# Third LayerNorm and pre-norm in one pass over the un-normed sum, with four projections multiplied before the norm and corrected when they are copied out

## The chip, the cores and the metric

The kernel runs on one core of a Trainium2 chip. The metric is the device time of one launch in microseconds (us); the time of a version is the median of its runs. Five engines work from queues of their own, each in program order: TensorE (PE, with its weight loads listed as PEld), VectorE (DVE), ScalarE (ACT), GpSimd (POOL) and SyncE (SP, which here only issues loads). They wait for each other by semaphores.

## The reference, cut to what matters

Two transformer blocks follow each other on 256 tokens of 1024 channels. The change lies at the seam.

```python
def layer_norm(x, g, b):
    xf = x.astype(f32)
    mu = xf.mean(-1, keepdims=True)
    var = jnp.square(xf - mu).mean(-1, keepdims=True)
    return ((xf - mu) * lax.rsqrt(var + EPS) * g.astype(f32) + b.astype(f32)).astype(x.dtype)
...
def rms_norm(x, g):
    x32 = x.astype(jnp.float32)
    y = x32 * lax.rsqrt(jnp.mean(x32 * x32, axis=-1, keepdims=True) + NORM_EPS)
    return (y * g.astype(jnp.float32)).astype(x.dtype)
...
        h = conv_ffn(x, ffn_w_up[l], ffn_conv_w[l], ffn_conv_b[l], ffn_w_down[l])
        x = layer_norm(ALPHA * x + h, ln3_g[l], ln3_b[l])
...
    h = rms_norm(x, g_pre_mix) * (1 + scale1) + shift1
    (sc_b, sc_c, sc_x, q, k, v, z, xbc, dt_raw,
     gl_a, gl_b, gl_c) = split_columns(h @ w_in)
```

`shift1` and `scale1` are columns of a modulation `silu(c) @ mod_w + mod_b`.

## The kernel before, in words

Activations lie with channels on the partitions and the 256 tokens along the columns: `X` is eight k-tiles of 128 x 256. Every large product is made from float32r halves: an operand is split into a rounded high half and the low rest, and `three` (L415) issues three matmuls, high by high, low by high, high by low. One unit of a linear (`linears_g`, L435) makes 256 output channels: 8 k-tiles x 2 column halves x 3 matmuls of 256 columns, 48 in all, into one of three PSUM banks (`lin`); five other banks (`att`) rotate for everything else.

Weights come through a plan (L187 to L291), a list of 512 KB pieces in the order of their use. `load` (L309) puts a piece into one of six raw buffers by SP. `stage` (L337) makes its halves: the high one on ScalarE (`hir`), the low one on VectorE (`lor`), in four buffers of each. `take` (L381) stages up to three pieces ahead of the one that PE is about to use, as far as buffers are free. Between weight pieces the plan carries 48 modulation pieces (`add_mod`); each is one multiply with a sum over 1024 columns on VectorE (`mod_step`, L331). All helpers append to the queue of an engine at once (`Queue.do`, L64), so the order of the Python code is the order of each engine's work, and a wait blocks what stands behind it on that engine alone.

The first block ends with eleven gated units "up" (convolution, gelu, product, split by `hid_put`) and four units "down" of 22 k-tiles (L1137 to L1140). After each "down" unit `resid` adds the result to `X`, and `stats` collects sums and squares. Then `layer_norm` (L1166) runs: `finish` (L932) turns the sums into mean and 1/deviation on small tiles and spreads them over the partitions with a diagonal and a matmul by ones; `apply` (L963) subtracts, scales, squares for the next norm and writes `X`. `pre_norm` (L1180) does the same for the RMS norm and splits the result h1 into high and low halves in `INH` and `INL`. Only then can PE start the units of the second block: q and k together (L1212), the small dt product (L1217), v, xs0, xs1, bc with a convolution of 2.4 us on VectorE behind each of the last three, scc, scx (L1276 to L1282), scb, z0, z1, and then the attention and scan stage with the gate units as filler.

Of the kernel before, what the change touches and what calls it, by code (L numbers as in the profile page):

```python
# [93 lines left out]
def build(nc, A, out):  # L94
    with ExitStack() as ctx:
# [14 lines left out]
        INH = sb("INH", 2048, F32R)[:, :].rearrange("p (k t) -> p k t", t=T)  # L110
        INL = sb("INL", 2048, F32R)[:, :].rearrange("p (k t) -> p k t", t=T)
# [149 lines left out]
        for c in range(4):  # L261
            add(("down", c), A["ffn_w_down"], 256 * c, 22, mod=3, spread=True)
# [4 lines left out]
        for n in ("v", "xs0", "xs1", "bc", "scc", "scx", "scb", "z0", "z1"):  # L267
            add((n, 2), w2, P2[n], 8, mod=int(n[0] in "sz"))
# [886 lines left out]
        def square3(k, n, d, t):  # L1155

            b = k // 2 % 2
            s_ = SQ[:, b, (k % 2) * T:(k % 2 + n) * T].rearrange("p (b t) -> p b t", t=T)
            for i in range(n):
                h = act(s_[:, i, :], d[:, i, :], ACT.Square, t, *sqf[b], scale=V("ln3_g", k + i), bias=V("ln3_b", k + i))  # L1160
            if k % 2 or n == 2:
                fold()
                sqp["fold"] = k // 2, h
            return h
# [498 lines left out]
```

How the kernel before makes its waits and increments, by code:

```python
    def wait(self, *tokens):  # L53
        need = {}
        for t in tokens:
            if t is not None:
                k = id(t[0])
                if t[1] > self.seen.get(k, 0) and t[1] > need.get(k, (None, 0))[1]:
                    need[k] = t
        for k, (sem, v) in need.items():
            self.seen[k] = v
            self.todo.append(lambda e, s=sem, v=v: e.wait_ge(s, v))
# [1 line left out]
    def do(self, fn, *tokens, inc=True):  # L64
        self.wait(*tokens)
        if not inc:
            self.todo.append(fn)
            return None
        self.n += 1
        self.todo.append(lambda e: fn(e).then_inc(self.sem, 1))
        return (self.sem, self.n)
# [101 lines left out]
        def dma(o, i, *w, s=None, q=None):  # L173
            if s is None:
                nsem[0] += 1
                s = sem(f"s_d{nsem[0]}")
            q = q or SP
            q.wait(*w)
            q.todo.append(lambda e: e.dma_start(o, i).then_inc(s, 16))
            return (s, 16)
```

## Time and profile before

| what | value |
|---|---|
| median of 3 runs | 922.96 us (922.44 to 923.41) |
| the profiled execution's own time | 921.22 us |
| its span, first to last instruction | 919.4 us |
| mean granted TensorE clock | 0.960 of full |
| busy: PE, DVE, ACT | 859.9, 647.6, 486.9 us |
| moved by DMA | 166.40 MB, 181 GB/s on average |

The rows further down are read so: in a timeline the first number is the start in us from the beginning of the span, the second the time to the end of the last instruction of a merged group, `out<-in` are the tiles, `xN` the number of instructions, and the bracket tells how long the engine was idle before and what ended that. Durations of neighbours overlap a little, so the distance of two starts is the better measure of what one costs.

### The profile page before, as it was taken

How to read it: one execution, taken by the hardware profiler on the slowest of the kernel's cores; microseconds unless marked ns; L12 is line 12 of the kernel's file. 1: busy time of each engine (PE TensorE's matmuls, PEld its weight loads, DVE VectorE, ACT ScalarE, POOL GpSimd, SP SyncE). 2: the span in 40 equal slices, each digit the busy share in tenths (PEclk: the TensorE clock that was granted, in tenths of full speed). 3: DMA queues.
4: the chain of work that ended last, by engine and by line, in shares of the span. 5: the costliest groups of instructions: out<-in, count | busy, mean ns of one | idle time of the engine just before them, and what ended most of it. 6: DMA issues, size and time to landing. Idle time of an engine off the chain costs nothing.

```text
span 919.4 us, 16216 instructions
## 1 busy us (share of the span) xinstructions
PE 859.9 (94%) x6578; PEld 821.4 (89%) x6578; DVE 647.6 (70%) x986; ACT 486.9 (53%) x680; POOL 6.2 (1%) x15
## 2 busy tenths in 40 slices
PE   5999998989889999999968999999996999999995
PEld 5889986879779999999967999898995999999995
DVE  4775777688678877787766696677877766655443
ACT  5644447444445666654435646788654544444450
POOL 0200000000000000000000000000000000000000
PEclk9999999989999999999977999999997899999998
DMA  9774556846052766569851485564664377765531
GB/s 332 219 234 124 180 180 190 250 155 229 25 161 91 218 185 180 182 189 318 267 182 46 134 264 167 143 187 142 219 192 138 104 240 230 228 208 170 178 111 47
DMA packets 145578, 166.40 MB, mean 181 GB/s; under 512 B 5488, under 2 KB 135536, under 8 KB 145504
## 3 DMA queue, kind: packets, MB, share of 16 engines
q1 hardware_dynamic: 143888, 162.82, 57.0%
q0 software_dynamic: 544, 1.49, 0.7%
q8 instruction: 52, 0.85, 0.4%
q10 hardware_dynamic: 1072, 1.05, 0.3%
q14 instruction: 22, 0.18, 0.1%
HBM read 164.10 MB, written 1.25 MB: 180 GB/s over the span
## 4 chain that ended last, share of the span: by engine, by line
PE 71%; DVE 8%; ACT 4%; issue 1%; DVEq 0%; ACTq 0%
PE ps L166 48%; PE ps L421 22%; DVE X L145 2%; ACT FA L142 2%; DVE lor L145 1%; DVE FA L145 1%; ACT hir L142 1%; ACT L142 1%; DVE FA L149 1%; DVE INL L145 1%; DVE st L145 0%; PE ps L169 0%; ACT SQ L142 0%; DVE X L153 0%; DVE SQ L145 0%
## 5 line engine op out<-in xcount | busy, mean ns | idle before, releaser
L166 PE MATMUL ps<-INH,hir 128*128 128x256 f32 x1320 | 384.4, 291 | 15.9 <-DVE lor L145 10.8
L145 DVE TENSOR_TENSOR lor<-raw,hir 128x1024 fp32r<-128x1024 f32 (+1 forms) x268 | 310.3, 1174 | 123.7 <-ACT hir L142 109.1
L421 PE MATMUL ps<-INL,hir 128*128 128x256 f32 x1320 | 379.4, 287 | 1.2 <-DVE INL L145 0.8
L166 PE MATMUL ps<-INH,lor 128*128 128x256 f32 x1320 | 378.7, 287 | 0.0
L142 ACT ACTIVATE hir<-raw 128x1024 fp32r<-128x1024 f32 (+1 forms) x268 | 266.9, 1015 | 143.4 <-PE ps L421 134.9
L166 PEld LDWEIGHTS ps<-INH,hir 128*128 128x128 f32 x1320 | 258.7, 196 | 23.8 <-issue 11.8
L421 PEld LDWEIGHTS ps<-INL,hir 128*128 128x128 f32 x1320 | 258.4, 196 | 2.8 <-DVE INL L145 2.8
L166 PEld LDWEIGHTS ps<-INH,lor 128*128 128x128 f32 x1320 | 258.8, 196 | 1.1 <-issue 1.0
L166 PE MATMUL ps<-HIH,hir 128*128 128x256 f32 x608 | 173.7, 286 | 0.2 <-DVE lor L145 0.2
L166 PE MATMUL ps<-HIH,lor 128*128 128x256 f32 x608 | 172.0, 283 | 0.0
L421 PE MATMUL ps<-HIL,hir 128*128 128x256 f32 x608 | 172.0, 283 | 0.0
L166 PEld LDWEIGHTS ps<-HIH,hir 128*128 128x128 f32 x608 | 116.6, 192 | 2.1 <-issue 1.2
L166 PEld LDWEIGHTS ps<-HIH,lor 128*128 128x128 f32 x608 | 116.7, 192 | 0.5 <-issue 0.5
L421 PEld LDWEIGHTS ps<-HIL,hir 128*128 128x128 f32 x608 | 116.7, 192 | 0.0
L153 DVE SCALAR_TENSOR_TENSOR FA<-ps,vec,FA 128x254 f32<-128x254 f32 (+2 forms) x130 | 53.2, 473 | 20.9 <-ACT FA L142 20.7
L142 ACT ACT_TABLE_LOAD x43 | 55.2, 1283 | 8.6 <-DVE small L156 5.5
L334 DVE SCALAR_TENSOR_TENSOR raw<-raw,cb 128x1024 f32<-128x1024 f32 x48 | 58.2, 1218 | 0.0
L142 ACT ACTIVATE FA<-ps,vec 128x256 f32<-128x256 f32 x58 | 29.4, 558 | 40.4 <-PE ps L421 40.4
L142 ACT ACTIVATE FA<-ps 128x512 f32<-128x512 f32 x47 | 27.4, 594 | 36.9 <-PE ps L421 30.7
L166 PE MATMUL ps<-FA 128*128 128x256 f32 (+6 forms) x212 | 39.2, 365 | 3.5 <-DVE FA L145 2.7
L142 ACT ACTIVATE HIH<-FA 128x512 fp32r<-128x512 f32 (+2 forms) x34 | 21.3, 628 | 39.3 <-DVE FA L145 17.4
L145 DVE TENSOR_TENSOR HIL<-FA,HIH 128x512 fp32r<-128x512 f32 (+2 forms) x34 | 23.4, 689 | 23.0 <-ACT HIH L142 22.9
(128 smaller groups left out, 634.6 us busy)
## 6 DMA issues: line engine op xcount, KB each, us to landing
raw<-in_w_in SPq DMA_DIRECT2D x64, 512.0 KB, 4.6
raw<-in_mod_wT SPq DMA_DIRECT2D x48, 512.0 KB, 4.5
raw<-in_ffn_w_up SPq DMA_DIRECT2D x44, 512.0 KB, 4.5
raw<-in_w_ffn_in SPq DMA_DIRECT2D x44, 512.0 KB, 4.7
raw<-in_ffn_w_down SPq DMA_DIRECT2D x20, 512.0 KB, 4.8
raw<-in_w_ffn_out SPq DMA_DIRECT2D x20, 512.0 KB, 3.4
raw<-in_xa_wkv SPq DMA_DIRECT2D x16, 512.0 KB, 4.0
raw<-in_xa_wq SPq DMA_DIRECT2D x8, 512.0 KB, 5.3
```

Of the source, the lines that this page charges most:

```text
L142: return AC.do(lambda e: e.activation(o, i, f, **kw), *w)
L145: return DV.do(lambda e: e.tensor_tensor(o, a, b, op), *w)
L149: return DV.do(lambda e: e.tensor_scalar(o, a, s1, None, op0), *w)
L153: return DV.do(lambda e: e.scalar_tensor_tensor(out=o, in0=a, scalar=s, in1=b, op0=op0, op1=op1), *w)
L166: return PE.do(lambda e: e.matmul(o, l, r, start=start, stop=stop, skip_group_check=True), *w, inc=inc)
L334: return DV.do(lambda e: e.scalar_tensor_tensor(out=w, in0=w, scalar=1.0, in1=CB[:, :], op0=ALU.mult, op1=ALU.mult, accum_out=col), t, t_sc)
L421: return PE.do(lambda e: e.matmul(o, *b, start=False, stop=stop, skip_group_check=True), inc=stop)
```

## The change

The statistics of the sum `ALPHA*x + h` now serve both norms: besides sum and square sum, products with the LayerNorm's gain and bias give the RMS of the normed result by algebra (`sums`, `rows3`). While the "down" units run, each tile of `X` is scaled by the combined gain (`GG`) and split into `INH` and `INL` un-normed, with four extra columns (gain, bias, shift) behind the 256 (`put_scaled`, `vector`). The units q, k, scc and scx multiply that (`late_g`; each holds two banks), and are corrected when they are copied out: `centre` subtracts the mean's share and scales by 1/deviation, `settle` applies the RMS factor and the shift. The true h1 is still made for dt, v and all later units (`h1_put`, `h1_low`), now in `HIH` and `HIL`. The units scc and scx move ahead of dt and v; six modulation pieces move from the "down" units to the kv units, and two from scc and scx to xs0 and xs1. The small constants and one matmul that sums three of them over the partitions come ahead of the "down" units.

The diff, cut to its core (`diag` is the first half of `spread`, and `steps_of` runs a number of a generator's steps):

```diff
+        INHX = sb("INH", 8 * TE, F32R)[:, :].rearrange("p (k t) -> p k t", t=TE)
+        INLX = sb("INL", 8 * TE, F32R)[:, :].rearrange("p (k t) -> p k t", t=TE)
+        INH, INL = INHX[:, :, 0:T], INLX[:, :, 0:T]
         HIH = sb("HIH", 22 * T, F32R)[:, :].rearrange("p (k t) -> p k t", t=T)
         HIL = sb("HIL", 22 * T, F32R)[:, :].rearrange("p (k t) -> p k t", t=T)
         SQ = sb("SQ", 1024)[:, :].rearrange("p (a n) -> p a n", a=2)
-            add(("kv", c), A["xa_wkv"], 256 * c, 8, mod=1)
+            add(("kv", c), A["xa_wkv"], 256 * c, 8, mod=2)
-            add_wide(("kv", 4 + c), A["xa_wkv"], 1024 + 512 * c, 8, mod=2)
+            add_wide(("kv", 4 + c), A["xa_wkv"], 1024 + 512 * c, 8, mod=3)
-            add(("down", c), A["ffn_w_down"], 256 * c, 22, mod=3, spread=True)
+            add(("down", c), A["ffn_w_down"], 256 * c, 22, mod=2 - c % 2, spread=True)
-        for n in ("v", "xs0", "xs1", "bc", "scc", "scx", "scb", "z0", "z1"):
-            add((n, 2), w2, P2[n], 8, mod=int(n[0] in "sz"))
+        for n in ("scc", "scx", "v", "xs0", "xs1", "bc", "scb", "z0", "z1"):
+            add((n, 2), w2, P2[n], 8, mod=int(n in ("xs0", "xs1", "scb", "z0", "z1")))
...
+        class Late(Inp):
...
+            def put_scaled(self, k, src, g, *w):
+                a = act(self.hi[:, k, 0:T], src, ACT.Copy, *w, *self.free, scale=g)
+                self.tok[k] = (a, stt(self.lo[:, k, 0:T], src, g, self.hi[:, k, 0:T].bitcast(F32), ALU.mult, ALU.subtract,
+                                      a, *w, *self.free))
...
+        def late_g(keys, x):
...
+            bs = []
+            for c in range(len(keys)):
+                bs.append([])
+                for p in (lin, att):
+                    bs[c].append(p.get())
+                    bs[c][-1].held = True
+            done = [None] * len(keys)
+            PE.wait(*x.ext)
+            for k0 in (0, HALF):
+                ws = [weights(key, k0) for key in keys]
+                for k in range(HALF):
+                    kk = k0 + k
+                    for c, (h, hi, lo, ta, tb) in enumerate(ws):
+                        PE.wait(ta, tb, x.tok[kk][0])
+                        for j, b in enumerate(bs[c]):
+                            if kk == 0:
+                                PE.wait(*b.free)
+                            cs = slice(128 * j, 128 * j + 128)
+                            done[c] = three(b.ap[:, 0:T + x.n], hi[:, k, cs], lo[:, k, cs], x.hi[:, kk, 0:T + x.n],
+                                            x.lo[:, kk, 0:T + x.n], kk == 0, kk == 7, x.tok[kk][1])
+                        if k == HALF - 1:
+                            hfree[h] = [done[c] if kk == 7 else PE.do(PE.todo.pop())]
+                    if kk < 7:
+                        yield
+            return list(zip(bs, done))
-        for c in range(4):
-            b, t = linear(("down", c), 22, hid)
-            t = resid(c, b, t)
-            t = stats(c, X[:, 2 * c:2 * c + 2, :], t, True)
...
-        t_x3 = layer_norm("ln3_g", "ln3_b", None, t, square3)
...
         t_gm = stt(GM[:, 0:8], MOD[:, 8:16], 1.0, V("g_pre_mix", n=8), ALU.add, ALU.mult, mod_bias(0, 16))
...
-        h1 = Inp(INH, INL)
+        tt(GG, g3, GM[:, 0:8], ALU.mult, t_gm)
+        t_gg = tt(BG, b3, GM[:, 0:8], ALU.mult)
+        stt(G2, g3, 1.0 / 1024, g3, ALU.mult, ALU.mult)
+        stt(GBN, g3, 1.0 / 1024, b3, ALU.mult, ALU.mult)
+        DV.do(lambda e: e.memset(MV, 1.0 / 1024))
+        copy(MV[:, :, 1], G2[:, 6:8], DV.now())
+        copy(MV[:, :, 2], GBN[:, 6:8])
+        stt(CH[:, 0:8], b3, 1.0 / 1024, b3, ALU.mult, ALU.mult)
+        DV.do(lambda e: e.tensor_reduce(CST[:, 0:1], G2, AX, ALU.add), DV.now())
+        DV.do(lambda e: e.tensor_reduce(CST[:, 1:2], GBN, AX, ALU.add))
+        t_cs = DV.do(lambda e: e.tensor_reduce(CST[:, 2:3], CH[:, 0:8], AX, ALU.add))
...
+        xg = Late(INHX, INLX, 4)
+        xg.free = [PE.now()]
+        xg.vector(0, GG.unsqueeze(2), t_gg)
+        xg.vector(1, BG.unsqueeze(2), t_gg)
+        xg.vector(2, MOD[:, 0:8].unsqueeze(2).to_broadcast([128, 8, 2]), t_gg)
...
+        at[0] = base + 12
...
+        def col(m, j, n, lhs, rhs, first, last):
+            return mm(Y3[:, m, j:j + n], lhs[:, m * 128:(m + 1) * 128], rhs, start=first, stop=last, inc=last)
...
+        b = att.get()
+        t_cs = copy(CST, b.ap[:, 0:3], mm(b.ap[:, 0:3], C("ones"), CST, t_cs, *b.free, inc=True))
...
+        for c in range(4):
+            b, t = linear(("down", c), 22, hid)
+            t = resid(c, b, t)
...
+            q = act(sq, xc, ACT.Square, t, *sqf[int(c > 0)])
+            for i in range(2):
+                g = act(qg[:, i, :], xc[:, i, :], ACT.Square, t, t_g, *ph, scale=V("ln3_g", 2 * c + i))
+            if c < 3:
+                for i in range(2):
+                    k = 2 * c + i
+                    for dst, co in ((A1, G2), (A2, GBN)):
+                        if k:
+                            t_a = stt(dst, X[:, k, :], co[:, k:k + 1], dst, ALU.mult, ALU.add, t, DV.now())
+                        else:
+                            t_a = ts(dst, X[:, k, :], co[:, k:k + 1], None, ALU.mult, None, t, t_cs, *ph)
...
+            if c in (1, 2):
+                t_q = tt(SQ[:, 0, :], SQ[:, 0, :], SQ[:, 1, :], ALU.add, q, t_q)
...
+                prev = X[:, 0:2, :] if c == 1 else XS_SUM
+                t_m = tt(XS_SUM, prev, xc, ALU.add, t, t_m, *sumf[0])
+                t_g = tt(QGA, QGA, QGT, ALU.add, g)
...
+            if c == 3:
+                q3, g3_, x3_ = q, g, t
+            for k in (2 * c, 2 * c + 1):
+                xg.put_scaled(k, X[:, k, :], GG[:, k:k + 1], t, t_gg)
...
+        def sums():
+
+            PE.wait(*sb3.free, t_q, t_m, t_s, t_a, t_con)
+            for m in range(2):
+                col(m, 0, 1, st[:, 0, :], o1024, m == 0, False)
+                col(m, 1, 1, A1, ones1, False, False)
+                col(m, 2, 1, A2, ones1, False, False)
+                col(m, 3, 1, SQ[:, 0, 0:T], o1024, False, False)
...
+            PE.wait(x3_)
+            for m in range(2):
+                for i in range(2):
+                    col(m, 0, 3, X[:, 6 + i, :], MV[:, i, :], False, False)
...
+            PE.wait(q3, g3_)
+            for m in range(2):
+                for i in range(2):
+                    col(m, 3, 1, SQ[:, 1, i * T:(i + 1) * T], o1024, False, False)
+                    t = col(m, 4, 1, QGT[:, i, :], o1024, False, i == 1)
...
+        def rows3(t):
...
+            a = copy(y, Y3, t)
+            sb3.free, sb3.held = [a], False
+            a = tt(mm2, m_, m_, ALU.mult, a)
+            a = stt(e_, e_, LN_EPS, mm2, ALU.add, ALU.subtract, a)
+            a = ts(e_, e_, LN_EPS, None, ALU.max, None, a)
+            a = act(s0, e_, ACT.Sqrt, a)
+            tm = diag(m_, 0)
...
+            a = recip(r, s0, a)
+            tr_ = diag(r, 1)
...
+            a = ts(p_, p_, RMS_EPS, None, ALU.max, None, c)
+            a = act(s0, p_, ACT.Sqrt, a)
+            recip(r2, s0, a)
+            return tm, tr_, r2
...
+        def rows_out(ts_):
+
+            b = att.get()
+            PE.wait(*b.free)
+            for i in range(2):
+                t = mm(b.ap[:, i * T:(i + 1) * T], C("ones"), DG[:, i, :, :].rearrange("p m n -> p (m n)"), ts_[i], inc=i == 1)
+            dgf[0] = dgf[1] = [t]
+            t = act(st[:, 0:2, :], wide2(b.ap), ACT.Copy, t)
+            b.free = [t]
+            return t
...
+        h1 = Inp(HIH[:, 8:16, :], HIL[:, 8:16, :])
...
-        pre_norm(0, 0, h1, sqp["t"])
+        g = late_g([("q", 2), ("k", 2)], xg)
+        steps_of(g, 2)
+        t_sum = sums()
+        tm, tr_, r2 = rows3(t_sum)
+        steps_of(g, 3)
+        t_rows = rows_out((tm, tr_))
+        t_r2 = diag(r2, 0)
+        t_d = []
+        for c in range(4):
+            xc, d = X[:, 2 * c:2 * c + 2, :], HB[:, 2 * c:2 * c + 2, :]
+            t = tt(d, xc, over(MB, 2), ALU.subtract, t_rows, *ph)
+            t = tt(d, d, over(RB, 2), ALU.mult, t)
+            t_d.append([act(X[:, k, :], HB[:, k, :], ACT.Identity, t, t_vec, scale=V("ln3_g", k), bias=V("ln3_b", k))
+                        for k in (2 * c, 2 * c + 1)][1])
...
+            if c == 0:
+                steps_of(g, 1)
+                b2 = att.get()
+                b2.held = True
+                t_r2 = mm(b2.ap[:, 0:T], C("ones"), DG[:, 0, :, :].rearrange("p m n -> p (m n)"), t_r2, *b2.free, inc=True)
+                dgf[0] = [t_r2]
+                R2 = b2.ap[:, 0:T]
+        units = run(g)
...
+        def centre(i, unit, dst):
...
+            bs, t = unit
...
+            for j, b in enumerate(bs):
+                a = copy(vs[j], b.ap[:, T:T + 3], t)
+                a = stt(dst[:, j, :], MB, vs[j][:, 0:1], b.ap[:, 0:T], ALU.mult, ALU.subtract, a, t_rows, *ph)
+                b.free, b.held = [a], False
+            return vs, tt(dst, dst, over(RB, 2), ALU.mult, a)
+
+        def settle(vs, a, dst):
+
+            for j in range(2):
+                a = stt(dst[:, j, :], dst[:, j, :], vs[j][:, 1:2], R2, ALU.subtract, ALU.mult, a, t_r2)
+                t = act(dst[:, j, :], dst[:, j, :], ACT.Identity, a, scale=-1.0, bias=vs[j][:, 2:3])
+            return t
...
+        def h1_put(c):
...
+            d = HB[:, k:k + 2, :]
+            a = tt(d, X[:, k:k + 2, :], over(R2, 2), ALU.mult, t_d[c], t_r2)
+            for i in range(2):
+                h = act(h1.hi[:, k + i, :], HB[:, k + i, :], ACT.Identity, a, t_gm, *h1.free,
+                        scale=GM[:, k + i:k + i + 1], bias=MOD[:, k + i:k + i + 1])
+            for i in range(2):
+                x = act(HB[:, k + i, :], HB[:, k + i, :], ACT.Identity, a, scale=GM[:, k + i:k + i + 1], bias=MOD[:, k + i:k + i + 1])
+            return h, x
...
+        def h1_low(c, h, x):
...
+            t = tt(h1.lo[:, k:k + 2, :], HB[:, k:k + 2, :], h1.hi[:, k:k + 2, :].bitcast(F32), ALU.subtract, h, x, *h1.free)
+        SCX = SCB
+        late = late_g([("scc", 2)], xg)
+        steps_of(late, 2)
+        cq = [centre(i, units[i], dst) for i, dst in enumerate((Q2, K2))]
+        p0 = h1_put(0)
+        p1 = h1_put(1)
+        h1_low(0, *p0)
+        p2 = h1_put(2)
+        h1_low(1, *p1)
+        units = run(late)
+        late = late_g([("scx", 2)], xg)
+        steps_of(late, 2)
+        cs_ = centre(2, units[0], SCC)
+        p3 = h1_put(3)
+        h1_low(2, *p2)
+        h1_low(3, *p3)
+        t_q2 = settle(*cq[0], Q2)
+        t_k2 = settle(*cq[1], K2)
+        units = run(late)
-        two = linears([("q", 2), ("k", 2)], 8, h1)
-        t_q2 = ev("q", Q2, got=two[0])
-        t_k2 = ev("k", K2, got=two[1])
+        t_scc = settle(*cs_, SCC)
+        t_scx = settle(*centre(3, units[0], SCX), SCX)
+        b2.held, b2.free = False, [DV.now()]
-        b, t = linear(("scc", 2), 8, h1)
-        t = copy(SCC, wide2(b.ap), t)
-        b.free = [t]
-        b, t2_ = linear(("scx", 2), 8, h1)
-        t = tt(SCC, SCC, wide2(b.ap), ALU.mult, t, t2_)
-        b.free = [t]
+        t = tt(SCC, SCC, SCX, ALU.mult, t_scc, t_scx)
-        mg = Inp(HIH[:, 8:16, :], HIL[:, 8:16, :])
+        mg = Inp(INH, INL)
```

## Rows read from the trace of the kernel before

**Rows 1.** The page, busy time, share and instruction count of each engine.

```profile
PE 859.9 (94%) x6578; PEld 821.4 (89%) x6578; DVE 647.6 (70%) x986; ACT 486.9 (53%) x680; POOL 6.2 (1%) x15
```

**Rows 2.** Table by windows: us, busy (instructions) per engine, granted clock, DMA share, GB/s.

```profile
460.00:470.00 10.00, 9.63 (x82) 9.55 (x80) 5.12 (x6) 3.19 (x3) 0.00 (x0) 1.00 0.96 307
470.00:480.00 10.00, 4.74 (x16) 3.75 (x16) 7.99 (x20) 4.07 (x7) 0.00 (x0) 0.55 0.37 110
480.00:490.00 10.00, 5.80 (x20) 4.45 (x20) 6.28 (x18) 7.41 (x15) 0.00 (x0) 0.50 0.00 0
490.00:500.00 10.00, 10.00 (x68) 10.00 (x67) 8.18 (x17) 5.44 (x9) 0.00 (x0) 0.76 0.01 2
```

**Rows 3.** Timeline (start, us, engine, line, instruction, idle before), up to down.

```profile
405.20 0.28 PE L421 MATMUL ps<-INL,hir 128*128 128x256 f32 x1
405.32 0.28 PE L166 MATMUL ps<-HIH,hir 128*128 128x256 f32 x1
...
407.56 1.65 DVE L153 SCALAR_TENSOR_TENSOR FA<-ps,vec,FA 128x255 f32<-128x255 f32 x4
...
410.70 0.69 DVE L145 TENSOR_TENSOR HIL<-FA,HIH 128x512 fp32r<-128x512 f32 x1 [0.70 <-ACT HIH L142]
```

**Rows 4.** Timeline of the end of the down stage.

```profile
468.68 0.50 PE L166 MATMUL ps<-con,st 128*128 128x1 f32 x4
...
469.80 0.68 DVE L153 SCALAR_TENSOR_TENSOR X<-X,ps 128x512 f32<-128x512 f32 x1
...
471.05 1.04 ACT L142 ACTIVATE hir<-raw 128x1024 fp32r<-128x1024 f32 x1
...
472.90 0.17 DVE L940 TENSOR_REDUCE small<-ps 128x4 f32<-128x8 f32 x1 [1.30 <-PE ps L166]
473.10 0.16 DVE L145 TENSOR_TENSOR small<-small 128x2 f32<-128x2 f32 x1
...
475.70 0.41 DVE L145 TENSOR_TENSOR X<-X,ps 128x256 f32<-128x256 f32 x1
```

**Rows 5.** Timeline of the pre-norm and of the first q and k matmuls.

```profile
480.72 1.40 DVE L145 TENSOR_TENSOR X<-X,ps 128x512 f32<-128x512 f32 x2
...
483.15 2.06 ACT L142 ACTIVATE X<-X,vec 128x256 f32<-128x256 f32 x4
...
486.13 1.22 PE L166 MATMUL ps<-st,con 128*128 128x256 f32 x2 [1.36 <-DVE st L145]
...
488.50 0.58 PE L166 MATMUL ps<-INH,hir 128*128 128x256 f32 x1 [1.15 <-ACT INH L142]
...
490.07 0.41 PE L166 MATMUL ps<-INH,lor 128*128 128x256 f32 x1
...
490.29 0.41 PE L421 MATMUL ps<-INL,hir 128*128 128x256 f32 x1
...
494.91 0.28 PE L166 MATMUL ps<-INH,hir 128*128 128x256 f32 x1
...
495.03 0.28 PE L166 MATMUL ps<-INH,lor 128*128 128x256 f32 x1
```

**Rows 6.** Timeline of VectorE from 495 to 570.

```profile
498.12 2.36 DVE L145 TENSOR_TENSOR lor<-raw,hir 128x1024 fp32r<-128x1024 f32 x2 [1.61 <-ACT hir L142]
...
502.66 1.41 DVE L156 COPY FA<-ps 128x512 f32<-128x512 f32 x2 [2.19 <-PE ps L421]
...
511.94 0.69 DVE L156 COPY FA<-ps 128x512 f32<-128x512 f32 x1 [0.44 <-PE ps L421]
...
544.50 0.17 DVE L156 COPY small<-ps 128x32 f32<-128x32 f32 x1
544.61 0.62 DVE L149 TENSOR_SCALAR FA<-FA,vec 128x256 f32<-128x256 f32 x2
...
546.72 1.21 DVE L145 TENSOR_TENSOR lor<-raw,hir 128x1024 fp32r<-128x1024 f32 x1
```

**Rows 7.** The chain in order of time, attention stage: start, us, what.

```profile
150.66 1.73 DVE FA L149 x7
```

More of the change, by code:

```diff
@@ L494, in wide_g, with __init__, vector, steps_of @@
             return list(zip(bs, done))
+        class Late(Inp):
+            def __init__(self, hi, lo, n):
+                super().__init__(hi, lo)
+                self.n, self.ext = n, []
+            def put_scaled(self, k, src, g, *w):
+                a = act(self.hi[:, k, 0:T], src, ACT.Copy, *w, *self.free, scale=g)
+                self.tok[k] = (a, stt(self.lo[:, k, 0:T], src, g, self.hi[:, k, 0:T].bitcast(F32), ALU.mult, ALU.subtract,
+                                      a, *w, *self.free))
+            def vector(self, i, src, *w):
+                h = self.hi[:, :, T + i:T + i + src.shape[2]]
+                a = act(h, src, ACT.Copy, *w, *self.free)
+                b = tt(self.lo[:, :, T + i:T + i + src.shape[2]], src, h.bitcast(F32), ALU.subtract, a, *w, *self.free)
+                self.ext = [a, b]
+        def late_g(keys, x):
[24 more added lines that the diff above has]
+            return list(zip(bs, done))
+        def steps_of(g, n):
+            for _ in range(n):
+                next(g)
         def linear(key, kt, x, outs=None):
@@ L1153, in build @@
         sqp = {"fold": None}
[L1155 to L1164, printed above, removed]
-        t_x3 = layer_norm("ln3_g", "ln3_b", None, t, square3)
@@ new lines, in build @@
+        t_cs = DV.do(lambda e: e.tensor_reduce(CST[:, 2:3], CH[:, 0:8], AX, ALU.add))
[5 more added lines that the diff above has]
+        at[0] = base + 12
+        A1, A2 = fa(1), fa(1)
+        QGA, QGT = fat(2), fat(2)
+        HB = fat(8)
+        ph = [PE.now(), DV.now(), AC.now()]
+        sb3 = att.get()
@@ new lines, in h1_put @@
+        def h1_put(c):
+            k = 2 * c
+            d = HB[:, k:k + 2, :]
[6 more added lines that the diff above has]
+            return h, x
@@ L1191, in build @@
+        def h1_low(c, h, x):
+            k = 2 * c
+            t = tt(h1.lo[:, k:k + 2, :], HB[:, k:k + 2, :], h1.hi[:, k:k + 2, :].bitcast(F32), ALU.subtract, h, x, *h1.free)
+            for i in range(2):
+                h1.tok[k + i] = (h, t)
         at[0] = base2 = 0
@@ L1523, in post, with pre_norm @@
             return outs
+        hb_free = [[], []]
+        def pre_norm(gi, si, inp, t):
+            _, br = finish(False, RMS_EPS, t)
+            for fn in sqp.pop("rest", ()):
+                fn()
+            apply(None, br, lambda k, n: X[:, k:k + n, :], lambda k, n: HB[:, k % 4:k % 4 + n, :],
+                  lambda k: GM[:, gi + k:gi + k + 1], lambda k: MOD[:, si + k:si + k + 1], inp, t_gm, dfree=hb_free, ready=t_x3)
         t_md = mod_bias(16, 40)
```

57 lines of the change are left out of this document (41 added, 16 removed).

## The prediction

> **What bounds the kernel now.** I read the page first: TensorE (PE) is busy 94% of the span [rows 1], so nearly every microsecond is matmul work at a fixed pace, and a change can win only where PE waits or runs at its lower clock. The table by windows says where that is: full before 460, then down to 4.74 and 5.80 of 10 us at a granted clock of 0.55 and 0.50 (the 1.2 GHz level), full again after 500 [rows 2]. This hole is the third LayerNorm and the pre-norm. The timelines give its edges: the last "down" matmul is done at 468.8, where the statistics' small matmuls follow [rows 4]; the first q matmul starts at 488.50, and until 494.8 PE runs at the half clock, one 256-column matmul each 0.21 us instead of 0.12 [rows 5]. q and k are copied out at 502.66 [rows 6]. Two units of 48 matmuls at 0.12 are 11.5 us; from 468.8 to 502.6 are 33.8, so the hole costs 22.3 us. That is all there is to win here.
>
> **What it puts there.** q and k now multiply the un-normed sum, so PE goes on at 468.8. 24 late matmuls at 0.12 end at 471.7. The 22 statistics matmuls that follow (4 in 0.50 [rows 4]) end near 474.5: the residual add (469.80, as before), the 512-wide square and the two scaled squares (0.49 each, four in 2.06 [rows 5]) are done by 472.1, in time. k-tiles 2 to 4 run to 478.8, the two spreads (1.22 each at the half clock [rows 5], so 0.6) to 480.0, the rest with the R2 spread to 486.4, scc to 492.3; scx gets q's bank near 493.5 and ends near 499.4. The columns grow from 256 to 260: no row shows 260; the nearest is 0.12 at 256, and a 512-column one would cost about twice that. I take 0.122; even at 0.23 PE would end the four units only near 518, about where the next step lies anyway.
>
> **The next wait.** The dt matmuls are next on PE, and they wait for the split of w_dt, which is queued on ScalarE (ACT) and VectorE (DVE) behind everything that makes h1. DVE's queue from the copy of the statistics (475.3: k's second low half has to be made first, after ACT's squares) to that split holds:
> - the row chain: 16 small operations at 0.2 (472.90 to 473.10 [rows 4]) and two diagonals at 0.42, 4.1 us with the square roots between;
> - 7 low halves of weights (scc, scx, v twice each, xs0 once) at 1.14 (two in 2.36 [rows 6], the second starting 1.14 on): 8.0;
> - one diagonal 0.4; 8 normalising operations on 512 columns at 0.62 (two in 1.40 [rows 5], the second dependent): 5.0;
> - 3 centrings (two small copies 0.2, two 256-wide on PSUM 0.41 [rows 4], one 512-wide 0.6): 5.6;
> - 4 h1_put and 4 h1_low at 0.61: 4.9; 4 settle operations at 0.36: 1.5; the split 0.25.
>
> That is 29.7 us. Between them DVE waits for ACT, which has 8 X writes and 16 h1 writes at 0.49, 4 settles and the weights' high halves at 1.04 [rows 4] in its own order. Walking both queues: X writes end 488.9, scx's high halves 490.8, so DVE waits 2.0 for the first; h1_low(0) waits 1.5, h1_low(1) 0.75; v's high half stands behind h1_put(2)'s four writes, 2.25; h1_low(3) 1.45; xs0's high half behind the settles, 2.0; scc's first 0.7. That is 10.7, so the split is done at 475.3 + 29.7 + 10.7 = **515.7**. PE waits from 499.4, over 16 us, and its clock falls as in the hole of today.
>
> ScalarE has one price that no row shows alone: a write with a scale column but no bias column. I use 0.49, a row with both. The Trainium skill (ScalarE: Activation LUTs, What ACT_TABLE_LOAD costs) says that each per-partition pointer operand adds about 93 ns. By it the four such writes ahead of k's high half would cost 0.40 each, and the sum would be 0.4 us lower; no run here shows it.
>
> **Sum for this stage.** Today v is copied out at 511.94 [rows 6], 9.3 us after q and k, and scc and scx (11.5 us) are still to come: 523.5 as the comparable point. Afterwards v ends at 515.7 + 9.3 + 2.8 = 527.8; the 2.8 is the half clock (6.3 us at 0.21 instead of 0.12 [rows 5]). xs0 then takes the bank of scx (three linear banks in rotation), which is freed only when DVE, after the copy of v (0.65) and scc's settle (0.7), has centred its first half (0.6): 2.0. So 529.8 against 523.5: **+6.3**. The hole is not closed; it moves behind scx. Bounds: -13 (dt starts when PE is ready, at 499.4: xs0 at 510.7) to +10.
>
> **The constants' sum.** A new matmul adds three constants over the partitions. It is issued before the first "down" matmul, and PE executes in order, so the whole "down" stage stands behind it. It waits for the third of three reductions on DVE, and these are queued behind the last gated unit. Today PE goes from "up" to "down" without a pause (405.20, 405.32), while DVE does the last convolution from 407.56, then the product, and the low half from 410.70 [rows 3], ending at 411.3. Thirteen small operations follow (two lines of modulation, seven products and fills, a square, three reductions): 1.4 to 2.7 us by 0.11 each (544.50 to 544.61 [rows 6]) to 0.2 (where one needs the one before [rows 4]); I take 2.3. PE stands from 405.5 to 413.6, the matmul itself 0.3, and the clock has fallen: 8.6 + 2.8 = **+11.4** (9.5 to 13). Nothing gives this back: PE is full in the "down" stage.
>
> **Later units.** scc and scx no longer stand between the convolutions and scb, and they were DVE's slack. Today z0's second low half runs from 546.72 [rows 6] to 548.0, 36.0 after v's end. PE needs it after six units and a half, 6 x 5.76 + 2.88 = 37.4: slack 1.4. Afterwards PE needs it after four units and a half plus the bank wait, 27.9. DVE drops 4 low halves (4.6), scc's copy (0.6), and does one modulation column before v's end (1.15), but adds scc's settle, scx's centring and settle (3.3): 33.0. It is 5.1 late; DVE's own waits shrink a little; I take **+4.5** (0 to 7).
>
> **Moved columns.** Six modulation steps (as wide as a low half, so 1.14 on DVE; 512 KB each) go from "down" to the kv units. "down" gains nothing, as PE is full there. In the attention stage DVE has room, except where its normalising is on the chain (150.66 [rows 7]); one extra step falls right ahead of it: **+1.2** (0 to 4). Each also takes a turn of the six raw buffers on SP's queue; that is in the upper bound. The new squares, the A1 and A2 sums and the un-normed halves in "down" add some 5 us to DVE at each unit's end; weights are staged three half units (8.6 us) ahead, so about **+0.3** (0 to 2).
>
> **Total**: 6.3 + 11.4 + 4.5 + 1.2 + 0.3 = +23.7. The profiled execution took 921.22 (span 919.4) and would take 944.9; the median of the runs is 1.7 higher, 922.96, so I say **946**, rounding down for the unproven waits.
>
> **Rivals.**
> 1. Only the constants' wait counts (20%). ACT and DVE interleave better than my walk, dt starts at 499.4, and the stage gives -12.8 instead of +6.3: 922.96 + 11.4 - 12.8 + 4.5 + 1.5 = 928; halfway, with dt at 508, 936. For it: the 10.7 us of waits between the two queues are walked, not read. Against: 29.7 us of DVE's own work alone end at 505.
> 2. Faster (7%): the corrections stay wholly behind PE. The place is dt's first matmul. If it starts at 499.4 with the clock kept, if scx's bank is free by v's end, and if DVE is not late at z0, the stage gives -14.8; with the constants' wait at its lower bound of 9.5 the time is 917.7. It decides only if dt starts before about 502 and z0 never waits; DVE's own work speaks against that.
> 3. Worse (6%): the moved columns reach the attention chain several times (4), DVE holds z0 by 7, the stage costs 10: 922.96 + 13 + 10 + 7 + 4 + 2 = 959.
>
> No change within 0.2% (1.8 us, about what a measurement of this kernel can tell) needs rival 1 with z0's wait gone: 3%.
>
> **How the numbers follow.** The forecast has 64%, and with the bounds of its terms 938 to 956 of its own. Rival 1 reaches down to 928; the range 931 to 956 leaves out rivals 2 and 3, no change, and the lowest part of rival 1, under 2 in 10. Slower: 64 + 20 + 6 = 90%; faster 7%, same 3%.
>
> **What would show it.** Right: PE idle for 8 us between the last "up" and first "down" matmul, with a matmul of 3 columns waiting for a reduction, then half clock; PE dense across the end of "down"; a second gap of 10 to 16 us ahead of dt, ended by the low half of w_dt, again at half clock; xs0 waiting for a DVE operation on PSUM. Wrong: no gap at "down", or dt following scx at once, or q and k still starting after the statistics.

## Result and the profile after

The changed kernel takes **951.8 us** (median of 4 runs, 950.7 to 952.6) against 922.7 for the kernel before: a ratio of 1.032 (95% interval 1.030 to 1.033), 29 us slower. 946 (931 to 956) was predicted. The profiled execution took 951.63 with a span of 949.8, 30.4 more than that of before.

First the page's busy times, and the table by windows around the two places where PE now waits (columns as in [rows 2]):

```profile
PE 863.2 (91%) x6592; PEld 824.7 (87%) x6592; DVE 663.4 (70%) x1038; ACT 497.8 (52%) x708; POOL 6.2 (1%) x15
```

```profile
410.00:420.00 10.00, 3.14 (x27) 2.93 (x25) 9.07 (x21) 3.39 (x7) 0.00 (x0) 0.87 0.64 207
420.00:430.00 10.00, 9.29 (x65) 9.29 (x65) 4.08 (x13) 2.90 (x6) 0.00 (x0) 0.79 0.24 67
480.00:490.00 10.00, 10.00 (x87) 10.00 (x86) 4.82 (x6) 4.22 (x8) 0.00 (x0) 1.00 0.92 299
490.00:500.00 10.00, 10.00 (x61) 10.00 (x61) 5.05 (x20) 2.08 (x5) 0.00 (x0) 0.66 0.24 70
500.00:510.00 10.00, 10.00 (x81) 9.84 (x80) 7.96 (x11) 6.57 (x12) 0.00 (x0) 1.00 0.34 105
510.00:520.00 10.00, 8.87 (x72) 8.52 (x71) 7.33 (x15) 4.06 (x7) 0.00 (x0) 1.00 0.35 107
520.00:530.00 10.00, 0.15 (x2) 0.00 (x0) 6.94 (x12) 5.96 (x11) 0.00 (x0) 0.66 0.28 77
530.00:540.00 10.00, 2.75 (x14) 1.67 (x15) 6.29 (x11) 5.68 (x11) 0.00 (x0) 0.50 0.21 62
```

PE's busy time hardly changed ([rows 1]); what it lost is idle time and clock. The hole of [rows 2] is gone where it was (480 to 500 is full) and stands at 520 to 540; a new one is at 410 to 420. The timeline names both, and the view of PE's waits from 480 to 640 gives their sums:

```profile
420.71 0.58 PE L168 MATMUL ps<-small,con 128*128 128x3 f32 x2 [7.58 <-DVE small L1228]
421.16 0.56 PE L168 MATMUL ps<-HIH,hir 128*128 128x256 f32 x1
...
486.11 0.28 PE L168 MATMUL ps<-INH,hir 128*128 128x260 f32 x1
486.23 0.28 PE L168 MATMUL ps<-INH,lor 128*128 128x260 f32 x1
...
537.25 0.38 PE L168 MATMUL ps<-HIH 128*8 128x256 f32 x1 [17.10 <-DVE HIL L147]
...
549.54 0.39 PE L168 MATMUL ps<-HIH,hir 128*128 128x256 f32 x1 [2.27 <-DVE FA L155]
```

```profile
PE ps L168 <- DVE HIL L147: 17.1, 1, 17.1
PE ps L168 <- DVE FA L155: 2.3, 1, 2.3
PE ps L171 <- DVE st L151: 1.8, 1, 1.8
PE ps L168 <- DVE small L158: 1.1, 1, 1.1
PE ps L168 <- DVE lor L147: 0.9, 2, 0.6
```

The late q matmuls follow the last "down" matmul at once, with 260 columns in the 0.12 of 256. The constants' matmul waits 7.58 for the last reduction (L1228), dt waits 17.10 for the low half of w_dt, xs0 waits 2.27 for scx's bank.

To compare executions I cut each at four points: **start** is the first of four matmuls of 4x256 early in the kernel (57.06 before), **kv** the statistics' matmul behind wout that waits 0.88 (194.87 before, 203.97 after), **T0** the end of "down" (468.68 before [rows 4], 486.11 after), then the end of the span. The start differs by up to 4 us between executions of kernels that are the same up to there (ScalarE waits 6.0 us for X's transfers in e12, 8.1 in the changed kernel), so it stands apart. All in us; ratios further down are against the kernel before as it ran beside each version (921.3 to 922.8):

| kernel | start | start to kv | start to T0 | T0 to end | median of runs |
|---|---|---|---|---|---|
| before | 57.1 | 137.8 | 411.6 | 450.7 | 922.7 |
| after | 59.2 | 144.8 | 426.9 | 463.7 | 951.8 |
| e1 constants later | 57.0 | 145.7 | 419.2 | 461.6 | 939.8 |
| e2 columns as before | 57.2 | 139.1 | 424.9 | 466.2 | 948.7 |
| e3 both | 57.5 | 139.1 | 418.1 | 462.2 | 940.7 |
| e4 before, columns moved | 56.8 | 146.0 | 420.3 | 449.1 | 927.8 |
| e5 e4, six steps left out | 57.0 | 139.8 | 414.3 | 449.1 | 922.9 |
| e6 e3, w_dt earlier | 59.4 | 137.6 | 415.4 | 459.3 | 934.1 |
| e7 only q and k late | 57.5 | 139.2 | 416.0 | 451.1 | 927.3 |
| e8 e1, columns to up | 55.5 | 139.0 | 412.5 | 464.2 | 935.2 |
| e9 before, kv columns to up | 58.1 | 137.3 | 411.5 | 449.0 | 917.9 |
| e10 e7, relieved | 57.7 | 137.8 | 411.4 | 448.3 | 918.3 |
| e11 after, mended | 57.2 | 136.2 | 410.2 | 457.7 | 929.1 |
| e12 e11, scx's bank earlier | 55.4 | 137.7 | 411.3 | 455.2 | 924.7 |

One of e6's four runs, at a granted clock of 0.736, took 1069.6 us, and its median is that of the other three.

A row is one execution, and executions of the same code differ: by 1.6 us from start to kv (137.6 to 139.2 in e2, e3, e6, e7, e8), by 2.7 up to T0 (e3, e6, e7), by 4.6 behind T0 (461.6 to 466.2 in the changed kernel, e1, e2, e3, e8) and by 1.7 there with the code of before (449.0 to 450.7 in before, e4, e5, e9). Smaller differences between two rows show nothing by themselves.

So the 30.4 us are 2.1 of start, **15.3** from start to T0 (7.0 of them up to kv) and **13.0** behind T0.

### The profile page after: what moved, and what is told of

Same layout as the page of the kernel before. It is cut to its first block, busy times and chain, and to the rows that moved or that the text cites. A ratio compares the mean times of both kernels' runs of the same rounds, so it can differ in the third digit from the quotient of the medians.

```text
span 949.8 us, 16312 instructions
## 1 busy us (share of the span) xinstructions
PE 863.2 (91%) x6592; PEld 824.7 (87%) x6592; DVE 663.4 (70%) x1038; ACT 497.8 (52%) x708; POOL 6.2 (1%) x15
## 4 chain that ended last, share of the span: by engine, by line
PE 66%; DVE 10%; ACT 6%; issue 2%; DMA 0%; DVEq 0%; ACTq 0%
PE ps L168 45%; PE ps L423 20%; ACT FA L144 2%; DVE lor L147 2%; DVE FA L147 2%; ACT hir L144 2%; DVE FA L155 1%; ACT L144 1%; DVE X L147 1%; DVE FA L151 1%; ACT HIH L144 1%; DMA raw<-in_xa_wkv 0%; PE ps L171 0%; DVE SQ L147 0%; ACT SQ L144 0%
## 5 line engine op out<-in xcount | busy, mean ns | idle before, releaser
L144 ACT ACTIVATE hir<-raw 128x1024 fp32r<-128x1024 f32 (+1 forms) x268 | 266.6, 1015 | 139.0 <-PE ps L423 132.8
L168 PE MATMUL ps<-INH,hir 128*128 128x256 f32 (+1 forms) x1096 | 318.2, 290 | 18.5 <-DVE lor L147 13.7
L423 PE MATMUL ps<-INL,hir 128*128 128x256 f32 (+1 forms) x1096 | 313.7, 286 | 0.4
L168 PE MATMUL ps<-INH,lor 128*128 128x256 f32 (+1 forms) x1096 | 312.8, 285 | 0.0
L168 PE MATMUL ps<-HIH,hir 128*128 128x256 f32 x832 | 242.0, 291 | 3.4 <-DVE FA L155 2.3
L168 PE MATMUL ps<-HIH,lor 128*128 128x256 f32 x832 | 238.0, 286 | 0.0
L423 PE MATMUL ps<-HIL,hir 128*128 128x256 f32 x832 | 237.9, 286 | 0.0
L168 PEld LDWEIGHTS ps<-INH,hir 128*128 128x128 f32 x1096 | 212.9, 194 | 23.8 <-issue 11.5
L168 PEld LDWEIGHTS ps<-INH,lor 128*128 128x128 f32 x1096 | 212.6, 194 | 1.0 <-issue 1.0
L423 PEld LDWEIGHTS ps<-INL,hir 128*128 128x128 f32 x1096 | 212.1, 194 | 1.3 <-DVE INL L147 1.3
L168 PEld LDWEIGHTS ps<-HIH,hir 128*128 128x128 f32 x832 | 162.3, 195 | 8.0 <-issue 3.0
```

Of the source, the lines that this page charges most:

```text
L144: return AC.do(lambda e: e.activation(o, i, f, **kw), *w)
L168: return PE.do(lambda e: e.matmul(o, l, r, start=start, stop=stop, skip_group_check=True), *w, inc=inc)
L423: return PE.do(lambda e: e.matmul(o, *b, start=False, stop=stop, skip_group_check=True), inc=stop)
```

## The experiments

**e1: the constants' matmul behind the first down unit.** In the changed kernel:

```
-        b = att.get()
-        t_cs = copy(CST, b.ap[:, 0:3], mm(...))
         for c in range(4):
             b, t = linear(("down", c), 22, hid)
             t = resid(c, b, t)
+            if c == 0:
+                b = att.get()
+                t_cs = copy(CST, b.ap[:, 0:3], mm(...))
```

> The changed kernel, but the matmul that sums the three constants is issued behind the first down unit instead of ahead of it, so that PE waits for no reduction of DVE there. Theory (the wait at the start of down is worth 9.7 us: T0, the end of down, lies 17.4 us later than before, of which 7.7 were there at the end of up): about 942, down starting within 0.3 us of the last up matmul, at full clock. Rival (PE would have waited there anyway, for the low half of the last gated unit or for weights, so the wait only changes its name): above 948, with a PE gap of several us still at the start of down.

939.8 us (ratio to before 1.019, interval 1.016 to 1.022). "Down" follows "up" at once, and the three-column matmul waits for nothing at 428.27. From kv to T0 it takes 273.5 where the changed kernel takes 282.1: 8.6 are gone, for the 9.7 expected. Behind T0 2.1 more went, with a shorter stretch at the half clock (last section). The median fell by 12.1; another 2.2 of that is the start in the profiles. The rival falls: PE had nothing else to wait for.

**e2, e3: the modulation columns planned as before**, without and with e1's edit:

```
-            add(("kv", c), A["xa_wkv"], 256 * c, 8, mod=2)
+            add(("kv", c), A["xa_wkv"], 256 * c, 8, mod=1)
-            add_wide(("kv", 4 + c), A["xa_wkv"], 1024 + 512 * c, 8, mod=3)
+            add_wide(("kv", 4 + c), A["xa_wkv"], 1024 + 512 * c, 8, mod=2)
-            add(("down", c), A["ffn_w_down"], 256 * c, 22, mod=2 - c % 2, spread=True)
+            add(("down", c), A["ffn_w_down"], 256 * c, 22, mod=3, spread=True)
```

> The changed kernel, but with the modulation columns planned as before (kv units 1 and 2 each, down units 3 each). Theory (every one of the six moved columns costs the kv stage its full DVE time of about 1.15 us): about 944.6, that is -7.2, and the kv stage level with the kernel before apart from the 1.9 us of the start. Rival A (my recorded +1.2 for the moved columns): about 950.6. Rival B (the down stage, whose DVE now also makes the un-normed halves and the sums, cannot take three columns a unit): 949 or more, with T0 no earlier than 486.0 less 3.

> Both edits of the two runs before together. Theory (the two costs lie one behind the other and add): about 935, -16.9 from the changed kernel; what is left, +12 over the kernel before, belongs to the third LayerNorm's stage and the units behind it. Rival (shared cost: down without the wait has DVE late, since six more columns stand there): 938 to 942.

e2 took 948.7 (1.029, 1.026 to 1.032), e3 940.7 (1.022, 1.018 to 1.026): both theories missed. e3's rival, a cost that "down" shares, came true; e2's rival B, of the same kind, was nearest, with T0 3.9 earlier for at most 3. The kv stage does get back 5.7 (144.8 to 139.1), but "down" now loses: in e3 its first unit waits 1.56 for a low half of weights, and the last one waits again, in the timeline:

```profile
415.92 0.36 PE L168 MATMUL ps<-HIH,hir 128*128 128x256 f32 x1 [1.56 <-DVE lor L147]
448.42 0.36 PE L168 MATMUL ps<-HIH,hir 128*128 128x256 f32 x1 [0.38 <-DVE lor L147]
466.89 0.55 PE L168 MATMUL ps<-HIH,hir 128*128 128x256 f32 x1 [2.40 <-DVE lor L147]
```

Since "down" also makes the un-normed halves and the sums, three columns a unit are too many for DVE there. So the columns cost nearly as much in "down" as in the kv units: e1 and e3 do not differ beyond their intervals.

**e4, e5: the columns alone, in the kernel before.** e4 makes the plan edit of the change and nothing else. e5 also puts a copy of one element a partition in the place of six DVE steps and leaves their transfers and buffers, so that six modulation columns are missing from its result:

```
+                if key[1] in (6, 8, 10, 12, 15, 18):
+                    rfree[s] = [copy(MOD[:, key[1]:key[1] + 1], raw[:, s * 1024:s * 1024 + 1], t)]
+                    return
                 rfree[s] = [mod_step(key[1], raw[:, s * 1024:(s + 1) * 1024], t)]
```

> The kernel before, with nothing changed but that six modulation columns go from the down units to the kv units. Theory (six full DVE steps on the chain of the kv stage): about 930, +7. Rival, the recorded term of my forecast (+1.2, DVE has room there): about 924. Second rival (the 1.9 us that the changed kernel is late at 85 us comes with the plan too, by another order of the transfers): the shift is there already at 85 us; if it is not, it belongs to something else in the change.

> The run that moved six modulation columns to the kv units in the kernel before, with six of the kv stage's modulation steps replaced by a copy of one element a partition; their transfers and raw buffers stay. It leaves out those six modulation columns. Theory (the columns cost VectorE's own 1.15 us each on the chain of the kv stage): the first statistics matmul after wout returns from 202.8 to within 1.5 us of 194.9, and the time to about 923. Rival (the raw buffers and SP's queue, a turn of which each column takes): it stays at 201 or later, the time at about 927.5.

e4: 927.8 (1.006, 1.004 to 1.009), start to kv +8.2, the median +5.0. e5: 922.9 (1.001, 1.000 to 1.003), start to kv +2.0. So most of the cost is DVE's own time. What e5 keeps is little more than the spread of 1.6, and its median is not clearly above the kernel before; a price of the raw buffers' turn is seen in one place and not shown as a quarter of the cost.

That place comes first, at 120 us: in e4 PE waits 1.55 for a DVE product, behind two pairs of modulation steps in DVE's queue (106 to 114 us) where the kernel before has two single ones and no wait, and then runs at the half clock from 122.4 to 125.7. By the distance of the same matmul from the start that is 3.3 of the 8.2. e5 still waits 1.15 there, because ScalarE's high half ahead of that product waits 2.65 for its transfer. PE in e4, then ScalarE and PE in e5:

```profile
120.63 1.13 PE L166 MATMUL ps<-FA 64*128 64x256 f32 x4 [1.55 <-DVE FA L145]
```

```profile
112.93 1.06 ACT L142 ACTIVATE hir<-raw 128x1024 fp32r<-128x1024 f32 x1 [2.65 <-DMA raw<-in_xa_wkv]
120.42 1.13 PE L166 MATMUL ps<-FA 64*128 64x256 f32 x4 [1.15 <-DVE FA L145]
```

Most of the rest comes at the attention's normalising, as the chain of waits shows; first e4, then e5 (start, us, what):

```profile
152.10 2.30 DVE raw L334 x5
154.40 1.14 DVE lor L145
...
156.08 1.74 DVE FA L149 x7
...
157.86 2.82 PE ps L169 x12
```

```profile
152.62 1.73 DVE FA L149 x7
154.36 0.04 issue
154.40 1.53 PE ps L169 x12
```

Two modulation steps (`raw L334`) stand on the chain ahead of the normalising of [rows 7], and PE's 12 matmuls behind it then run at 0.23 instead of 0.13 each: PE's wait is 3.75 for 1.84, and the clock is at its half level behind it. The waits from 148 us on and this clock add 2.4 us each. e4's start was not late, so the 2.1 of the changed kernel's start are not the plan's.

**e6: w_dt's split earlier**, on e3:

```
         h1_low(3, *p3)
+        wh, wl, tw = split("w_dt", PE.now())
         t_q2 = settle(*cq[0], Q2)
         t_k2 = settle(*cq[1], K2)
         units = run(late)
-        wh, wl, tw = split("w_dt", PE.now())
```

> The run with both undone (constants behind the first down unit, columns as before), and the split of w_dt taken ahead of the settling of q and k and of scx's end in the issue order. Theory (dt waits for nothing but DVE's queue up to that split): the first dt matmul comes 3.5 to 5 us earlier after the end of down than the 49.6 us of that run, and the time falls by 2 to 4, since the settling is then late for scx's bank. Rival (the lower halves of h1 hold dt anyway): under 1 us earlier, time unchanged at about 940.

934.1 (1.013, 1.011 to 1.016), 6.6 below e3; by the cuts 2.9 are behind T0 and 2.7 ahead of it, where the code is the same. In the trace:

```profile
522.61 0.38 PE L168 MATMUL ps<-HIH 128*8 128x256 f32 x1 [12.47 <-DVE HIL L147]
535.82 0.38 PE L168 MATMUL ps<-HIH,hir 128*128 128x256 f32 x1 [2.27 <-DVE FA L155]
```

PE's wait in front of dt is 4.6 shorter (12.47 for 17.08); dt comes 47.8 after T0 instead of 49.5, because this execution kept the low clock longer ahead of it (last section): DVE copies the statistics 10.4 after T0, for 7.9. Counted from that copy, dt starts 41.6 later in e3 and 37.4 in e6, 4.2 earlier, as the theory said; it is 41.6 to 42.4 in all five profiles with the split in its old place and 37.0 to 37.4 in the three with the new one (e6, e11, e12). So dt waits for its place in DVE's queue; the 12.5 that PE still waits are for what DVE does up to h1's last low half.

**e8: the six columns in six "up" units**, on e1 (two and one a unit stay in "down"):

```
-            add(("up", 11 + c), A["ffn_w_up"], 2816 + 256 * c, 8)
+            add(("up", 11 + c), A["ffn_w_up"], 2816 + 256 * c, 8, mod=int(c in (1, 3, 5, 6, 8, 9)))
```

> The changed kernel with the constants behind the first down unit, and the six columns taken neither by the kv units (planned as before) nor by down (two and one a unit, as in the changed kernel), but by six of the up units. Theory (the cost of a moved column hangs on DVE's slack where it lands; in the up units DVE is busy 16.2 of 20 us): first statistics matmul after wout at about 196.5, end of down at 469 to 470.5 against 476.1, time 933 to 935 against 939.8. Rival (six columns cost DVE's time wherever they go): end of down at 475 or later, time 939 to 940.

935.2 (1.015, 1.012 to 1.017), at the upper edge of the theory's 933 to 935. Start to T0 is 412.5, 6.7 less than e1 and 0.9 more than the kernel before: in the "up" units, where PE is full and DVE is not, the columns cost no more than the spread. (Behind T0 it took 2.6 more than e1; 1.3 of that lie ahead of dt, where its clock stayed low for longer.) It also shows that the new work in "down" costs nothing with three columns for two units.

**e9: the same place for the eight columns that the kernel before has in its kv units.**

> The kernel before with one edit: the eight modulation columns of its kv units go to eight of the up units. The runs so far say that six more columns in the kv units cost 7.9 us there and six in the up units nothing. Theory (the columns that stood in the kv units already are on the chain too): first statistics matmul after wout 3 to 8 us earlier than 194.9, the end of down as much earlier than 468.7, time 915 to 919.5. Rival (the kv stage had slack for the eight, only the extra ones hurt): within 1 us of 194.9 and time 922 to 923.

917.9 (0.997, 0.995 to 0.998): faster than before, inside the expected range, but not for the expected reason. Start to kv is 137.3 against 137.8: the rival was right there. PE's first matmul behind the normalising of [rows 7] came 2.2 us earlier from the start (151.32 - 58.10 = 93.2 against 95.4), but it then ran at the half clock until 154.6, and by kv the gain was 0.5. The profiled execution shows 1.8 in all apart from the start, and 1.7 of that behind T0, where e4 and e5, which have the same code there, show it too. Where the median's 3.7 come from stays open. Of e9's twelve runs the five at a granted clock of 0.960 took 919.8 to 921.8, the seven at 0.961 to 0.965 took 916.2 to 918.0; the profiled one is of the five, so its trace does not show what the median rests on.

**e7, e10: only q and k late.** e7 is e3 with scc and scx multiplied from h1 again, and h1 made tile by tile. e10 plans the columns as e9 does (ten in "up", four in o and skv, six in "down") and relieves both engines:

```
-            for i in range(2):
-                x = act(HB[:, k + i, :], HB[:, k + i, :], ACT.Identity, a, scale=GM[...], bias=MOD[...])
+            x = act(HB[:, k, :], HB[:, k, :], ACT.Identity, a, scale=GM[...], bias=MOD[...])
...
+            x = (x, ts(HB[:, k + 1, :], HB[:, k + 1, :], GM[...], MOD[...], ALU.mult, ALU.add, h))
```

> A version that keeps the idea for q and k alone, on the run with both undone: scc and scx are multiplied behind xs0, xs1 and bc from h1 as in the kernel before; the R2 diagonal follows the row chain at once, norm, put and low half of h1 are interleaved tile by tile, v comes ahead of dt, the centring of k and the settling behind the copy of v. Theory (DVE's queue ahead of the first product with h1 is what the four late units lengthen): v is copied out 35 to 38 us after the end of down, against 43.3 in the kernel before, and the time is 918 to 924. Rival (ACT's 24 writes and the row chain set it, whatever is late): v's copy no earlier than 43 after the end of down, time 928 or more.

> The version with q and k alone late, with the kv columns in ten up units and four earlier ones (o, skv), two and one a down unit; two tiles of h1 normalised and the first put before the weights of v are staged, and one of the two plain copies of each h1 pair made by VectorE instead of ScalarE. Theory (the late units' cover pays once DVE and ACT are relieved): v copied out 36 to 39 us after the end of down, against 43.3 before and 42.3 in the version without these edits; time 911 to 916. Rival (the cover pays nothing, the time is that of the plan alone): v's copy at 42 or later, time as the kernel before with its kv columns moved, or worse.

e7: 927.3 (1.006, 1.005 to 1.008), v copied 42.2 after T0, between theory and rival. e10: 918.3 (0.996, 0.995 to 0.998), v copied 38.9 after T0, as the theory expected, against 43.3 in the kernel before ([rows 4, 6]) and 42 in e4 and e9, which have that kernel's stage. The time was the rival's: T0 to end is 448.3 against the 449.0 to 449.1 of e4, e5 and e9, so nearly all of the 3.1 gained on e4 and e9 is given back: xs0 waits 1.62 for its bank, a later unit 1.47 for a low half, in e10's timeline:

```profile
509.33 0.39 PE L168 MATMUL ps<-HIH,hir 128*128 128x256 f32 x1 [1.62 <-DVE FA L155]
525.45 0.36 PE L168 MATMUL ps<-HIH,hir 128*128 128x256 f32 x1 [1.47 <-DVE lor L147]
```

Behind v both waits are for DVE, so an earlier v only makes PE wait there. e10 beats both kernels, by no more than e9's plan does alone.

**e11, e12: the changed kernel mended** (e6's edits and e10's plan), and e12 with the bank of scx freed earlier:

```
         units = run(late)
+        cx = centre(3, units[0], SCX)
+        t_scc = settle(*cs_, SCC)
...
         t_v2 = copy(V2, wide2(b.ap), t)
-        t_scc = settle(*cs_, SCC)
-        t_scx = settle(*centre(3, units[0], SCX), SCX)
+        t_scx = settle(*cx, SCX)
```

> The changed kernel with what the runs found mended (constants behind the first down unit, split of w_dt ahead of the settling) and the modulation columns planned as in the run beside it. Theory (what is left is the third LayerNorm's stage with four late units): first dt matmul 45 to 46.5 us after the end of down, xs0 still waiting for scx's bank, and 9 to 12 us lost from the end of down to the end against the kernel before; time 924 to 929. Rival (the stage's loss came from the queues' state at its start): under 5 lost there, time below 921.

> The mended version of the changed kernel, with the centring of scx and the settling of scc issued ahead of dt and v instead of behind the copy of v. Theory (xs0 waits for scx's bank because its centring stands behind that copy, and the later low halves are late by the DVE work that stands between): the 2.28 us in front of xs0 go, the waits for low halves behind shrink, and the time falls by 2 to 4 against the 929.1 of that version. Rival (DVE is late as a queue, whatever stands first): the wait turns into one for a low half of xs0's weights, time within 1 us.

e11: 929.1 (1.008, 1.006 to 1.011). dt comes 46.2 after T0 and xs0 waits 2.28 for its bank, as the theory expected; 7.0 are lost behind T0 (8.6 to 8.7 against e4, e5 and e9, whose code there is that of the kernel before): less than the theory's 9 to 12, more than the rival's 5, at a time just above the theory's. e12: 924.7 (1.005, 1.002 to 1.007), 4.4 less by the medians, 3.4 by the ratios, whose intervals overlap. The wait for the bank is gone, and more than half of it returns as a longer wait for a low half (3.21, for 1.84 in e11). Both sides have a part: the bank's term was real, and behind it DVE is late as a queue. With these terms mended the version is still 0.5% slower than the kernel before, and 0.8% slower than e9, which also has no modulation column in the kv units.

## Why the prediction was right

The direction, the size and the mechanism of the two large waits held. The constants came out 2.8 below the forecast and the moved columns 5.8 above it; that these partly cancel is luck. Without it the time would have been near 954.6, close to the upper end of the range.

- **Constants' sum, +11.4 (9.5 to 13): 8.6** from kv to T0 by e1, 9.3 by the rows (7.58, the matmul 0.45, the clock 1.3). It came out a little under the lower bound. The wait is the one described: DVE does the product, the low half at 418.43, then thirteen small operations to 420.7. PE stood 7.6 instead of 8.1. The half clock behind it was shorter than forecast: matmuls run at 0.21 from 421.16 to 424.1, some 14 of them, which costs 1.3 and not the 2.8 that was read from another hole.
- **The next wait, +6.3 (-13 to +10): +8.6.** dt starts 51.1 after T0, behind a gap of 17.1 where 10 to 16 was the sign; the split was forecast at 47.0. The walk through both queues was good: from the copy of the statistics to the end of the split, 40.4 forecast, 41.7 measured (495.27 to 537.0), of which 29.3 are DVE's own work, for 29.7, and the rest waits. Its start was not: the copy came 9.2 after T0 for 6.6. The 22 statistics matmuls are two instructions each in the trace, and the clock fell among them: 488.99 to 495.10, 6.1 instead of 2.8. The bank wait, forecast at 2.0, is 2.27 (and gone in e12). xs0 starts 63.4 after T0; the comparable point of before was 54.8.
- **Later units, +4.5 (0 to 7): 13.0 - 8.6 = 4.4.** The size came out, and DVE is late there because scc and scx no longer give it time, but not where the prediction put it: z0's second low half holds PE for 0.58, not 5.1 less a little. The longest of three waits, 1.84, stands ahead of scb, where small matmuls wait for dt's scan, which is queued on DVE behind the convolution of bc; none waits there in the kernel before. Another 1.6 are half clock behind the bank wait. That the sum is so near is in part luck.

```profile
566.02 0.36 PE L168 MATMUL ps<-HIH,hir 128*128 128x256 f32 x1 [0.34 <-DVE lor L147]
570.97 0.29 PE L171 MATMUL ps<-con,SQ 8*128 8x8 f32 x2 [1.84 <-DVE st L151]
580.78 0.35 PE L168 MATMUL ps<-HIH,hir 128*128 128x256 f32 x1 [0.58 <-DVE lor L147]
```


- **Moved columns, +1.2 (0 to 4): +7.0** up to kv in the changed kernel, +8.2 in e4 (+5.0 in its median). This step failed. It said that in the attention stage DVE has room except at the normalising, and that one step falls ahead of it. In e4 two stood there on the chain, two more delayed an earlier DVE product that PE needs at 120 us, and behind both waits PE ran at the half clock. DVE's busy share of that stage (16 of 20 us) was taken as room, though what stands ahead of PE is a queue in order.
- **"Down" gains nothing and pays 0.3.** e8 bears that out. What the prediction did not see is that the move protects "down": with three columns a unit there, e2 and e3 lose about as much.
- **ScalarE's price.** I took 0.49 for a write with a scale column and no bias, and named 0.40 as what the Trainium skill (ScalarE: Activation LUTs, What ACT_TABLE_LOAD costs) would give. Two such squares take 0.89 together in the timeline of the changed kernel, one alone 0.49, so the second starts 0.40 behind the first, where writes with both columns ([rows 5]) start 0.49 apart. The trace agrees with the page.

```profile
488.48 0.89 ACT L144 ACTIVATE FA<-X,vec 128x256 f32<-128x256 f32 x2
```

By the cuts the forecast had 1.5 up to kv and in "down", 11.4 for the constants and 10.8 behind T0; measured were 7.0 up to kv, 8.3 from there to T0, 13.0 behind: 28.3, and 2.1 of start. In e1, with less half clock, 10.9 lie behind T0. Rivals 1 and 2 needed dt to start by 508 on the forecast's scale, 39.3 after T0; it started 51.1 after, behind a wait of 17. Of rival 3 the mishap in the attention stage came, alone, at 7.0 for its 4.

## What to carry to other kernels

Six moved steps of 1.14 us cost 5 to 8 us here where their engine's queue stands ahead of the bound engine, and nothing beyond the spread where the bound engine is covered: look for the landing place by what waits behind it in order, not by the busy share. Taking work off the front of a serial stage helps only if the engine that makes the corrections has that time free; here PE waits for VectorE in the stage behind as well, so that cover in front was given back unit by unit. A small matmul that sums constants belongs behind a full unit: in front of one it held PE for 7.6 us.

## What was not expected of the hardware

PE's clock fell without PE being idle. Among the 44 matmuls of one to three columns the granted clock of the changed kernel goes from 1.00 to 0.50 (the 1.2 GHz level) at 492.4 and stays there until 499.1, though 260-column matmuls follow at 495.10. The table by windows of 1 us:

```profile
491.00:492.00 1.00, 1.00 (x11) 1.00 (x11) 0.79 (x1) 0.11 (x1) 0.00 (x0) 1.00 0.04 15
492.00:493.00 1.00, 1.00 (x9) 1.00 (x8) 0.44 (x1) 0.00 (x0) 0.00 (x0) 0.71 0.00 0
493.00:494.00 1.00, 1.00 (x6) 1.00 (x7) 0.00 (x0) 0.00 (x0) 0.00 (x0) 0.50 0.41 38
...
498.00:499.00 1.00, 1.00 (x7) 1.00 (x6) 0.66 (x4) 0.20 (x1) 0.00 (x0) 0.50 0.00 0
499.00:500.00 1.00, 1.00 (x9) 1.00 (x9) 0.07 (x1) 0.56 (x1) 0.00 (x0) 0.88 0.00 0
```

The same code kept the low level for 3 us in e1 (483.8 to 487.1) and for 10 in e2 (487.5 to 497.6). dt's start after T0 follows it (49.5 in e1, 51.1 here, 52.4 in e2), as does most of the spread of T0 to end among these three (461.6, 463.7, 466.2). In all ten profiles with these 44 matmuls the clock fell among them (the changed kernel, e2, e6, e7, e8, e11) or right behind the last of them (e1, e3, e10, e12), each time with PE dense. The fall costs several microseconds that differ from one execution to the next. No run has the late units without the tiny matmuls, so that these are the cause is not shown.
